# FFN first products with 512 moving columns: one load of the high weights meets the high and the low activations, and the two halves are joined outside TensorE

## The reference

```python
h = rms_norm(x, g)
# first block: z = conv3_causal(h @ w_in) + b, 2 x 2816 columns;  x += (gelu(gate) * up) @ w_out
# second block: a = conv3(h @ w_ffn_gate) + conv_b
#               x += (gelu(a) * (h @ w_ffn_up)) @ w_ffn_down
```

## Time and profile before

| | |
|---|---|
| median of 3 runs | 1573.98 us (1572.36 to 1575.08) |
| profiled execution, its span | 1573.1 us |
| TensorE matmul busy | 1546.2 us, 98% |
| VectorE busy | 1146.3 us, 73% |
| ScalarE busy | 909.9 us, 58% |
| GpSimd busy | 158.5 us, 10% |

### The profile page before, as it was taken

The page is one execution under the profiler, slowest core; times in us unless marked ns, Lnnn a source line. Parts: engine busy times, 40 slices in busy tenths (PEclk is TensorE's granted clock), DMA queues, the critical chain, the costliest instruction groups (busy, mean ns, idle before and its releaser), DMA issues.

```text
span 1573.1 us, 30181 instructions
## 1 busy us (share of the span) xinstructions
PE 1546.2 (98%) x12792; PEld 1498.9 (95%) x12792; DVE 1146.3 (73%) x1382; ACT 909.9 (58%) x1213; POOL 158.5 (10%) x91
## 2 busy tenths in 40 slices
PE   7999999999999999999999999999999999999998
PEld 7899999999999999899899999999889899999998
DVE  6768777888977788678458875678767647776666
ACT  6566545698666556456564744456645655644444
POOL 0211211100012110000031100010000013011010
PEclk9999999999999999999999999999999999999999
DMA  9345555444456545424245555544532334555552
GB/s 314 127 142 186 188 189 185 164 161 160 170 179 210 182 170 188 143 99 135 81 153 176 188 187 187 187 161 161 176 137 90 110 112 161 188 188 199 178 187 78
DMA packets 38412, 258.73 MB, mean 164 GB/s; under 512 B 4768, under 2 KB 5408, under 8 KB 7840
## 3 DMA queue, kind: packets, MB, share of 16 engines
q1 hardware_dynamic: 37872, 255.33, 47.1%
q10 hardware_dynamic: 432, 1.84, 0.3%
HBM read 256.10 MB, written 1.05 MB: 163 GB/s over the span
## 4 chain that ended last, share of the span: by engine, by line
PE 82%; issue 11%; ACT 3%; DVE 2%; POOL 1%; DMA 0%; SPq 0%; POOLq 0%; ACTq 0%; DVEq 0%
PE bank L1710 25%; PE bank L1711 24%; PE bank L1712 24%; PE bank L2018 3%; PE bank L1971 3%; PE bank L1990 2%; ACT w_hi L483 1%; PE bank L1941 1%; PE bank L1914 1%; DVE w_lo L990 1%; POOL y_lo L1632 0%; DMA x<-XT 0%; DVE h_lo L1005 0%; ACT h_hi L503 0%; ACT sq L641 0%
## 5 line engine op out<-in xcount | busy, mean ns | idle before, releaser
L1710 PE MATMUL bank<-h_hi,w_hi 128*128 128x256 f32 x2640 | 752.9, 285 | 12.4 <-DVE h_lo L1005 9.4
L1711 PE MATMUL bank<-h_lo,w_hi 128*128 128x256 f32 x2640 | 743.1, 281 | 0.0
L1712 PE MATMUL bank<-h_hi,w_lo 128*128 128x256 f32 x2640 | 742.3, 281 | 0.0
L990 DVE TENSOR_TENSOR w_lo<-raw,w_hi 128x2048 fp32r<-128x2048 f32 x237 | 550.7, 2326 | 171.3 <-ACT w_hi L483 170.5
L483 ACT ACTIVATE w_hi<-raw 128x2048 fp32r<-128x2048 f32 x237 | 452.9, 1912 | 239.9 <-PE bank L1712 239.9
L1710 PEld LDWEIGHTS bank<-h_hi,w_hi 128*128 128x128 f32 x2640 | 497.6, 189 | 24.6 <-issue 21.0
L1712 PEld LDWEIGHTS bank<-h_hi,w_lo 128*128 128x128 f32 x2640 | 501.0, 190 | 0.0
L1711 PEld LDWEIGHTS bank<-h_lo,w_hi 128*128 128x128 f32 x2640 | 497.2, 188 | 0.3
L1710 PE MATMUL bank<-y_hi,w_hi 128*128 128x256 f32 x1040 | 296.3, 285 | 7.0 <-POOL y_lo L1632 4.9
L1711 PE MATMUL bank<-y_lo,w_hi 128*128 128x256 f32 x1040 | 292.9, 282 | 0.0
L1712 PE MATMUL bank<-y_hi,w_lo 128*128 128x256 f32 x1040 | 292.7, 281 | 0.0
(11 more groups left out here) (227 smaller groups left out, 1343.4 us busy)
## 6 DMA issues: line engine op xcount, KB each, us to landing
raw<-W SPq DMA_DIRECT2D x237, 1024.0 KB, 4.9
raw<-W SPq DMA_DIRECT2D x4, 512.0 KB, 7.0
wide<-RW ACTq DMA_DIRECT2D x1, 1280.0 KB, 7.7
x<-XT SPq DMA_DIRECT2D x4, 256.0 KB, 6.1
OUT<-x SPq DMA_DIRECT2D x4, 256.0 KB, 2.0
wide<-CON SPq DMA_DIRECT2D x1, 768.0 KB, 9.3
val<-PE_T ACTq DMA_DIRECT2D x2, 256.0 KB, 2.7
vec<-VEC SPq DMA_DIRECT2D x1, 390.0 KB, 5.2
```

The source lines that it names most:

```text
L990: V.tensor_tensor(w_lo[:, n0 % NW], raw[:, n0 % NRAW], w_hi[:, n0 % NW].bitcast(F32), ALU.subtract)\
L1710: T.matmul(out, w[0], a[0], start=start, stop=False, **kw)
L1711: T.matmul(out, w[0], a[1], start=False, stop=False, **kw)
L1712: return T.matmul(out, w[1], a[0], start=False, stop=stop, **kw)
```

## The change

The eight banks become one tensor `acc`, and `h_hi` and `h_lo` become halves of one tensor `h`. In the FFNs' first products a 128-channel tile takes one whole bank. The high weights meet 512 columns at once (256 high, 256 low activations), and the low weights meet the 256 high ones and add to the second half of the bank. A unit then has 32 matmuls, 16 of 512 and 16 of 256 columns, and fills two banks: a always 4 and 5, b always 6 and 7. ScalarE copies the second halves to SBUF (`low_half`), VectorE adds the first halves (`joined`) and scales the sum in SBUF. TensorE waits, at a(s), for the join of a(s - 1), and at b(s) for that of b(s - 1). The sum of squares of an FFN stage goes to bank 2.

```diff
-            return (bank[4], bank[5]) if step % 2 == 0 else (bank[7], bank[6])
+            return acc[:, 4:6], acc[:, 6:8]
@@ ScalarE, ffn
+                def low_half(j, u, i):
+                    act.wait_ge(sems["w_used"], plus(u + 1 + j, i, 6))
+                    nc.scalar.activation(qk[:, 12 + 2 * j:14 + 2 * j], ff_banks()[j][:, :, S:2 * S], ACT.Copy)\
+                        .then_inc(sems["lows"], 1)
                 def step(s0, i=None):
+                    low_half(0, u, i)
                     if not late or not s0:
                         after(u, i)
...
                     elif causal:
                         after(u + 1, i)
                     if causal:
+                        low_half(1, u, i)
                         act.wait_ge(sems["scaled"], plus(c0 + 2 * s0 + 2, i, 4))
...
                     if late or not causal:
                         after(u + 1, i)
+                    if not causal:
+                        low_half(1, u, i)
@@ VectorE, ffn
+                def joined(j, s0, i):
+                    z, b = Z[:, 2 * j:2 * j + 2], ff_banks()[j]
+                    n = plus(2 * (FF_STEPS * f + s0) + j + 1, i, 4)
+                    dve.wait_ge(sems["lows"], n)
+                    V.tensor_tensor(z, b[:, :, 0:S], qk[:, 12 + 2 * j:14 + 2 * j], ALU.add).then_inc(sems["halves"], 1)
+                    dve.wait_ge(sems["halves"], n)
+                    V.tensor_tensor(z, z, rinv.unsqueeze(1).broadcast_to([P, 2, S]), ALU.mult).then_inc(sems["scaled"], 1)
...
-                    scale(ba)
+                    joined(0, s0, i)
...
-                    scale(bb)
+                    joined(1, s0, i)
@@ TensorE
+            def split_tile(n, t, out, ks=range(8)):
+                for k in ks:
+                    hi, lo = cols(n, k * 256 + t * 128, 128)
+                    T.matmul(out, hi, h[:, :, k], start=k == 0, stop=False, skip_group_check=True)
+                    m = T.matmul(out[:, S:2 * S], lo, h_hi[:, k], start=False, stop=k == 7, skip_group_check=True)
+                return m
...
-                        if s0 >= 2:
-                            if causal:
-                                pe.wait_ge(sems["cvu"], plus(FF_STEPS * causals.index(s) + s0 - 1, i, 2))
-                            else:
-                                pe.wait_ge(sems["cvg"], done(-1))
-                        column_tile(u, 0, ba[:, 0:S])
-                        column_tile(u, 1, ba[:, S:2 * S]).then_inc(sems["w_used"], 1)
+                        pe.wait_ge(sems["halves"], joined(-1))
+                        split_tile(u, 0, ba[:, 0])
+                        split_tile(u, 1, ba[:, 1]).then_inc(sems["w_used"], 1)
...
-                    if s0 >= 2:
-                        pe.wait_ge(sems["cvg" if causal else "ymul"], done(-1))
-                    elif s0 == 1:
+                    if s0:
+                        pe.wait_ge(sems["halves"], joined(0))
+                    if s0 == 1:
                         pe.wait_ge(sems["rms_done"], NORM[s] + 1)
```

More of the change, by code:

```diff
@@ L115, in sem @@
             return ctx.enter_context(nc.semaphore(name))
-        bank = [ctx.enter_context(nc.psum_tensor(f"bank{i}", [P, 512], F32)) for i in range(8)]
+        acc = ctx.enter_context(nc.psum_tensor("bank", [P, 8, 512], F32))
+        bank = [acc[:, i] for i in range(8)]
         raw = sb("raw", [P, NRAW, UW])
@@ L132, in build @@
         odr = sb("odr", [P, 4, 2])
-        h_hi = sb("h_hi", [P, DT, S], F32R)
-        h_lo = sb("h_lo", [P, DT, S], F32R)
+        h = sb("h", [P, 2, DT, S], F32R)
+        h_hi, h_lo = h[:, 0], h[:, 1]
         y_hi = sb("y_hi", [P, 2, 2, S], F32R)
@@ L191, in build @@
             pool_p pm_done psc sig_done bhi b_ready
-            tu tg cvu cvg gelu ymul yhi ffy
+            tu tg cvu cvg gelu ymul yhi ffy lows halves
             rgelu rexp rgin rtx xcv rmm rsig rth rm rsb rgy ryhi ry_ready
@@ L260, in scaled_before, with ff_banks, norm_bank @@
             return sum(SCALED[kind(a)] for a in used[:used.index(s)])
-        def ff_banks(step):
-            return (bank[4], bank[5]) if step % 2 == 0 else (bank[7], bank[6])
+        def ff_banks():
+            return acc[:, 4:6], acc[:, 6:8]
+        def norm_bank(s):
+            return bank[2] if kind(s) in ("ffn", "hf") else bank[6]
         def y_slot(step):
@@ L545, in norm @@
                 w = S + 2 if s in atts else S
-                nc.scalar.activation(rinv_t[:, 0:w], bank[6][:, 0:w], ACT.Sqrt, bias=eps, scale=1.0 / D)\
+                nc.scalar.activation(rinv_t[:, 0:w], norm_bank(s)[:, 0:w], ACT.Sqrt, bias=eps, scale=1.0 / D)\
                     .then_inc(sems["rms_done"], 1)
@@ L552, in ffn @@
                 nt, tap = (4, 2) if causal else (2, 1)
-                T = qk[:, 0:4, :]
+                T, Z = qk[:, 0:4, :], qk[:, 8:12, :]
                 c0 = scaled_before(s)
@@ L566, in step @@
                     late = parts_late(s, s0)
-                    up, gb = ff_banks(s0)
+                    low_half(0, u, i)
                     if not late or not s0:
@@ L575, in step @@
                         w, b = taps(t, s0, i)
-                        ins = nc.scalar.activation(T[:, t], up[:, t * S:(t + 1) * S], ACT.Identity, bias=b, scale=w)
+                        ins = nc.scalar.activation(T[:, t], Z[:, t], ACT.Identity, bias=b, scale=w)
                     ins.then_inc(sems["tu"], 1)
@@ L1144, in step @@
                     else:
-                        dve.wait_ge(sems["scaled"], plus(scaled_before(s) + 2 * s0 + 2, i, 4))
-                        up = bb[:]
+                        up = pair(qk, 5)
                     V.tensor_tensor(pair(qk, 3), pair(qk, 2), up, ALU.mult).then_inc(sems["ymul"], 1)
@@ L1732, in token_tile, with first_split_unit @@
                 return m
+            def first_split_unit(s, out):
+                n = ff_base(s)
+                unit(n)
+                for k in range(8):
+                    pe.wait_ge(sems["h_ready"], 4 * NORM[s] + k // 2 + 1)
+                    for t in range(2):
+                        m = split_tile(n, t, out[:, t], (k,))
+                m.then_inc(sems["w_used"], 1)
             def first_unit(s, out):
@@ L1779, in normed @@
                 pe.wait_ge(sems["sq_sum"], k + 1)
-                m = T.matmul(bank[6][:, 0:S], ones, sq[:, 0], start=True, stop=True)
+                if kind(s) == "hf":
+                    pe.wait_ge(sems["emb_ev"], 4 * ples_of(s) + 3)
+                m = T.matmul(norm_bank(s)[:, 0:S], ones, sq[:, 0], start=True, stop=True)
                 if s in atts:
@@ L1856, in step @@
                             embedding_sum(s)
-                    column_tile(u + 1, 1, bb[:, S:2 * S]).then_inc(sems["w_used"], 1)
+                    split_tile(u + 1, 1, bb[:, 1]).then_inc(sems["w_used"], 1)
                     if s0 and s0 < FF_STEPS - 2:
```

16 lines of the change are left out of this document (7 added, 9 removed).

## The result

The changed kernel takes 1604.74 us (median of 4 runs, 1601.87 to 1605.96) where the kernel before took 1574.53 beside it (4 runs, 1572.36 to 1576.21): a ratio of 1.0198, with a 95% interval of 1.018 to 1.0216. The profiled execution has a span of 1603.8 us, 30.7 more than before, at a mean granted clock of 0.991 (0.997 before).

The account below looks back on a forecast made before the run. TensorE was taken as the bound, its matmuls busy for 98% of the span. Terms -2.3 + 9.2 + 2.0 + 5.8 + 8.9 + 3.3 = +26.9 us on 1573.1 gave 1600.0 profiled; predicted 1600.5 us, range 1580 to 1613.

Parts of the forecast that it names:

- The likeliest case: Whole kernel: waits at stage starts and ends as worked out, 1588 to 1611 us; chance 67%.
- The gain (-2.3): TensorE's first-product units in four FFNs: each merged pair saves 1.6 ns, 2.3 us in all.
- The bound from a cost of the instruction (16.3): First-product units, upper bound: time beyond 106.7 ns is per instruction, so a merged pair saves 11.6 ns, 16.3 us in all.
- Starts of `hf` (+9.2): Start of `hf0` and `hf1`: a1 waits 1.6 us, b1 3.0, y0 4.6 later in each; 9.2 us.
- Start of `ffn0` (+2.0): Start of `ffn0`: y0 at 133.7 instead of 131.9, 0.2 us more by step 2; 2.0 us.
- Start of `ffn1` (+5.8): Steps 0 to 2 of `ffn1`: additions pile up, y3 at 480.4 instead of 474.6; 5.8 us.
- Ends (+8.9): End of `ffn0` and `ffn1`: y10 starts 4.4 us later for its low part; 8.9 us for both.
- The clock (+3.3): TensorE's granted clock falls after two of four new waits; 3.3 us, bounds 0 and 9.
- Steady steps: FFN loop: VectorE and ScalarE have room for the added work, so nothing waits; no gap.
- the faster wide product: Rival, first products: weight loads set 118.3 ns, wide and narrow take 320 ns, gain 49 us, 1554 in all; chance 9%.
- The hidden waits: Rival: only the starts of `hf0` and `hf1` still wait, +7 us, 1581; chance 10%.
- VectorE as the bound: Rival: low splits slip behind their units in every causal step, 8 us more, 1618 with upper-bound waits; chance 10%.

Follow-up runs that it names:

- experiment 2: Changed kernel, but in step 0 of both `hf` ScalarE copies b0's low half right after the first taps: 1599.47 us, ratio 1.0179.
- experiments 7 and 8: Changed kernel with VectorE's add but no ScalarE copy: 1588.2 us, ratio 1.0118; and with the copy but no add: 1588.1 us, ratio 1.0111.
- experiment 1: Changed kernel with each wide matmul split back into 256-column ones; banks, copies, adds and waits kept: 1610.52 us, ratio 1.0245.
- experiment 9: Changed kernel with copies, adds and splits reordered in step 0 of all FFNs and step 10 of the causal ones: 1580.34 us, ratio 1.0037.
- experiment 3: Changed kernel, but in step 10 of the causal FFNs b10 is copied and joined before y9's split, y10's split after y_hi: 1600.12 us, ratio 1.0186.
- experiment 5: Kernel before with bursts of extra, overwritten matmuls (wide ones or wide-narrow pairs) ahead of one unit in each FFN: 1572.4 us, one run.

## Why the prediction was right, and where its terms were off

The likeliest case happened: 1604.7 us for 1600.5, +30.7 for +26.9 in the profiled execution, inside 1580 to 1613, on the side that had 0.85. That the sum came so near is in part luck: 4.7 us that it didn't know of, from the y units, stood against 5 us that it put too low on the clock. (Its terms give 1600.9, not 1600.5; and the case's bounds, added up, give 1576 to 1614, wider than the 1588 to 1611 stated.)

- **The gain (-2.3).** It came as forecast: 353.3 ns a merged pair, 1.6 down, and 5.65 us a unit, for 5.64. The gain that came on top, 4.7 us, is the other order of the y units, of which the prediction knew nothing. The bound from a cost of the instruction (16.3) can be dropped: the time goes by columns. By the formula of the Trainium skill (TensorE: Matmul & The Clock Gate, section Back-to-back issue gap), which that section gives for single matmuls and not for a stream with weight loads, a wide and a narrow matmul would take 325 ns. The trace has 353.3 and doesn't agree.
- **Starts of `hf` (+9.2).** The waits were 1.6 and 2.6 us for a1 and b1 in both stages, against 1.6 and 3.0; experiment 2 shows that the copy behind gelu and split is the cause of b1's. What was missing is the clock behind it: from b1 to y0 8.50 and 7.22 us and not 5.68.
- **Start of `ffn0` (+2.0).** y0 at 133.66 where I had 133.7. But the clock stayed up this time, and the 1.6 us that the old y0 lost were given back. Then y2 waited 1.41 us (169.19), which the forecast had not, so that y3 was 1.6 us late, for 2.0.
- **Start of `ffn1` (+5.8).** +1.7 at y0 and +6.6 at y3. The piling up took place; experiments 7 and 8 give most of it to the add, on VectorE beside its tables: y2 and y3 wait 1.43 and 1.75 us with the add alone, 0.71 and 1.00 with the copy alone, as with neither.
- **Ends (+8.9).** From y8 to y10 it took 5.1 us more in `ffn0` and 6.4 in `ffn1` (1.6 of it the clock in y9), for 4.4 each. The missed link: y9's low split, behind the longer chain, was late as well (0.73 and 2.10 us).
- **The clock (+3.3).** Mis-sized. It cost 2.4 us in y10 of `ffn0`, 1.6 in each of y9 and y10 of `ffn1`, 2.8 and 1.5 at b1 of `hf0` and `hf1`: 9.9, less the 1.6 given back, some 8. I had let two of four new waits count; all four did, and y9's too.
- **Steady steps.** As worked out, no gap once the starts are over (y2 in `ffn0`, y3 in `ffn1`) but for 0.2 us in `hf1`: `hf0` needs 146.1 us from y0 to y8, and needed 147.8.

Of the rivals, the faster wide product fell with the 353.3 ns (it wanted 320, or 334 to break even), and experiment 1 has no more hidden in it. The hidden waits fell with the list of waits. VectorE as the bound was wrong for the steady steps, but right in small in `ffn1`'s first steps.

Open: why a stream of 256-column matmuls has two orders. That two pairs bring the faster one is shown for the places in step 2, not why one pair doesn't, or eight in `ffn0` didn't; one pair and eight were each seen in a single execution. What decides whether the clock falls after a wait is open as well.

## What to carry to other kernels

Merging two matmuls that share their weights saves next to nothing (here 1.6 ns of 354.9) where the stream's time already goes by columns: measure the wide form beside two narrow ones before paying other engines for it. An operation that is hidden in every steady step is paid at the first and last steps of a stage, where chains have no slack, and again in the clock that falls after the wait. Where a copy must stand in an in-order queue, put it ahead of the gelu and the splits that nobody waits for yet: moves of that kind (experiment 9) took back 25 of the 31 us here.

## What the hardware showed that I had not expected

- Streams of 256-column fp32r matmuls run at 118.3 or at 115.5 ns from start to start, at the same granted clock of 1.00, and keep their order over hundreds of matmuls until a wait. Behind units with wide matmuls, y units have 115.5; behind narrow ones 118.3, unless two pairs, a wait or chance changed it.
- A 512-column matmul takes the time of two 256-column ones (353.3 ns for wide and narrow, 354.9 for three narrow): one weight load less saved 1.6 ns. The order of a stream matters more: three narrow ones in the faster order take 346.5.
- The granted clock fell to its lower level after waits of TensorE of 2.1 us (y9 of `ffn0` in experiment 3, 152.3 ns a matmul), 2.57, 2.73, 3.5 and 4.27 us, and even 1.73 us (y3 of `ffn1` in experiment 9, 152.8 ns; the same wait left it up in the changed kernel), but not after 2.26 and 2.42 us, nor after 2.67 (y0 of `ffn0` with the add alone). Ahead of y0 of `ffn0` the wait was 1.83 us both in the kernel before, where the clock fell, and in experiment 5's, where it didn't (118.0 ns a matmul). The length of the wait alone doesn't tell it.
